# Four projections by rows of 256 columns become two of 512 in both mixers, the rotation two units sooner

## The reference

```python
for layer in range(DEPTH):                      # DEPTH = 2
    h = rms_norm(x, attn_norm_w[layer])
    proj = h @ w_in[layer]                      # 1024 -> 3072 columns, 12 slices of 256
    a_q, a_i, a_zf, a_zb, a_g, b_u, c_q, c_k, c_v = jnp.split(proj, SPLIT_POINTS, axis=-1)
    o_a = hgrn2_mixer(a_q, a_i, a_zf, a_zb, a_g, lb_all[layer])     # a chunkwise scan, 256 wide
    o_b = fourier_mixer(b_u)                                        # 2-D DFT, 256 wide
    o_c = dilated_attention_mixer(c_q, c_k, c_v, positions)         # rotary + attention, 512 wide
    x = x + jnp.concatenate([o_a, o_b, o_c], -1) @ w_out[layer]
    ...                                         # feed-forward
```

## Time and profile before

| | us |
|---|---|
| median of 3 runs | 2207.61 |
| lowest and highest run | 2207.59, 2208.95 |
| span of the profiled execution, first to last instruction | 2211.8 |
| PE busy in the span | 2148.4 (97%) |
| DVE, ACT, POOL busy | 1324.7, 949.9, 189.1 |

### The profile page before, as it was taken

The page is one execution under the profiler, slowest core; times in us unless marked ns, Lnnn a source line. Parts: engine busy times, 40 slices in busy tenths (PEclk is TensorE's granted clock), DMA queues, the critical chain, the costliest instruction groups (busy, mean ns, idle before and its releaser), DMA issues.

```text
span 2211.8 us, 32932 instructions
## 1 busy us (share of the span) xinstructions
PE 2148.4 (97%) x13984; PEld 1681.6 (76%) x13984; DVE 1324.7 (60%) x1976; ACT 949.9 (43%) x1442; POOL 189.1 (9%) x159
## 2 busy tenths in 40 slices
PE   8998999999999999999999999999999998999997
PEld 6885688888888785788888885676888567777775
DVE  8886555335437867455255453857433454888887
ACT  5445532222234347432223332345221234888885
POOL 1220000000001310100000200000000001122220
PEclk9999999999999999999999999999999998999999
DMA  5222033322222231222222221212110443799985
GB/s 187 69 80 77 20 119 119 119 101 97 102 85 77 72 96 39 76 83 102 102 96 95 96 96 55 77 53 82 59 59 32 144 168 125 292 349 364 358 346 217
DMA packets 55000, 275.69 MB, mean 125 GB/s; under 512 B 13142, under 2 KB 13398, under 8 KB 26048
## 3 DMA queue, kind: packets, MB, share of 16 engines
q1 hardware_dynamic: 45344, 264.32, 33.0%
q0 software_dynamic: 8928, 8.33, 1.1%
q10 hardware_dynamic: 576, 0.87, 0.1%
HBM read 268.31 MB, written 29.36 MB: 135 GB/s over the span
## 4 chain that ended last, share of the span: by engine, by line
PE 86%; DVE 7%; ACT 3%; DMA 1%; issue 1%; SPq 0%; POOL 0%; POOLq 0%; DVEq 0%; ACTq 0%
PE psum L123 83%; PE psum L126 3%; DVE A_mix L136 2%; ACT A_mix L130 1%; DVE WL L136 1%; DMA A_moe<-h_rows,A_moe 1%; ACT A_mix L133 1%; DVE A_second L136 1%; DVE A_mix L156 0%; DVE A_second L144 0%; DVE A_mix L162 0%; ACT WH L130 0%; SPq L168 0%; DMA A_mix<-A_mix 0%; DVE HL L136 0%
## 5 line engine op out<-in xcount | busy, mean ns | idle before, releaser
L136 DVE TENSOR_TENSOR WL<-raw,WH 128x1024 fp32r<-128x1024 f32 x236 | 300.9, 1277 | 351.6 <-ACT WH L130 351.2
L130 ACT ACTIVATE WH<-raw 128x1024 fp32r<-128x1024 f32 x236 | 247.5, 1054 | 357.6 <-PE psum L123 341.7
L123 PE MATMUL psum<-HH,WH 128*128 128x512 f32 x736 | 301.6, 410 | 17.5 <-DVE HL L144 10.1
L123 PE MATMUL psum<-R_op,WH 128*128 128x512 f32 x1024 | 316.0, 390 | 0.0
L123 PE MATMUL psum<-R_ffn,WH 128*128 128x512 f32 x1024 | 315.1, 389 | 0.0
L123 PE MATMUL psum<-HH,WL 128*128 128x512 f32 x736 | 290.3, 394 | 0.0
L123 PE MATMUL psum<-HL,WH 128*128 128x512 f32 x736 | 290.2, 394 | 0.0
L123 PEld LDWEIGHTS psum<-R_op,WH 128*128 128x128 f32 x1024 | 192.2, 188 | 40.6 <-issue 1.0
L123 PEld LDWEIGHTS psum<-R_ffn,WH 128*128 128x128 f32 x1024 | 192.2, 188 | 39.9
L123 PE MATMUL psum<-R_moe 128*128 128x512 f32 x800 | 198.3, 404 | 5.8 <-DVE ring_moe L136 3.4
L123 PE MATMUL psum<-R_ffn,WL 128*128 128x512 f32 x512 | 199.2, 389 | 0.0
(11 more groups left out here) (206 smaller groups left out, 3000.1 us busy)
## 6 DMA issues: line engine op xcount, KB each, us to landing
ring_moe<-in_w_gu SPq DMA_DIRECT2D x64, 1024.0 KB, 10.1
raw<-in_w_in SPq DMA_DIRECT2D x41, 1024.0 KB, 5.0
raw<-in_w_up SPq DMA_DIRECT2D x32, 1024.0 KB, 4.9
raw<-in_w_down SPq DMA_DIRECT2D x32, 1024.0 KB, 4.9
ring_moe<-in_w_dn SPq DMA_DIRECT2D x32, 1024.0 KB, 6.8
raw<-in_w_out SPq DMA_DIRECT2D x12, 1024.0 KB, 4.9
kept<-A_second SPq DMA_DIRECT2D x20, 256.0 KB, 2.6
A_mix<-A_mix SPq DMA_DIRECT2D x64, 64.0 KB, 2.0
```

Of the source, the lines that this page charges most:

```text
L123: return self.raw.matmul(o, l, r, start=start, stop=stop)
L130: return self.raw.activation(o, i, f, scale=scale)
L136: return self.raw.tensor_tensor(o, a, b, op)
```

## The change

The two halves of the row lins are joined: a_i and b_u become one lin of 512 columns, c_v another, with weights from a new array `w_row` that holds 4 x 128 rows by 512 columns in a chunk. The order of the mixer's lins is now four of `head` (units 0 to 7), c_q and c_k by columns (8 to 15), a_i with b_u (16 to 19), c_v (20 to 23). A tile of 128 positions fills one bank, so a row lin uses all four banks 0 to 3; in its last unit PE takes the tiles in the order 2, 3, 0, 1, and ACT reads them out in that order. `ROT` falls from 14 to 12. In `MIX` the scan's step kt moves behind two more half-units on ACT.

```diff
-                      lin([W[0, 0]], "silu", m.aq2, ly=ly), lin([W[4, 0]], "silu", m.ag2, ly=ly),
-                      lin([W[1, 0]], "rows", m.ai3, ly=ly)]
+                      lin([W[0, 0]], "silu", m.aq2, ly=ly), lin([W[4, 0]], "silu", m.ag2, ly=ly)]
...
-            m.tail += [lin([W[5, 0]], "rows", m.u3, ly=ly)]
-            m.tail += [lin([W[10 + j, 0]], "rows", m.cv3[:, :, 256 * j:256 * j + 256], ly=ly) for j in range(2)]
+            for j, to in enumerate(((m.ai3, m.u3), (m.cv3,))):
+                m.tail.append(lin([I["w_row"][ly, j, k] for k in range(2)], "rows", to, ly=ly))
...
-            for m in range(2):
-                b = (2 * (l.n - s2.low[0].n) + m) % 3 if l.kind in ("lat", "shift", "keep") else l.n % 2 * 2 + m
+            for m in range(4 if l.kind == "rows" else 2):
+                b = (2 * (l.n - s2.low[0].n) + m) % 3 if l.kind in ("lat", "shift", "keep") else (l.n % 2 * 2 + m) % 4
...
+        ROWS = (2, 3, 0, 1)
+
         def pe_rows(e, l):
...
+            us = [chunks[n][2] + h for n in l.chunks for h in range(2)]
+            for i, u in enumerate(us):
+                e.wait_ge(*at("w_lo", u))
+                wh, wl = unit(u)
+                final = u == us[-1]
+                order = ROWS if final else (0, 1, 2, 3)
+                for tk in order:
+                    if i == 0:
+                        clear(e, l, tk)
+                    o, ts = bank_of(l, tk), slice(tk * 128, (tk + 1) * 128)
+                    for k in range(2):
+                        xh, xl, made = operand(l, 2 * i + k)
+                        e.wait_ge(*at(*made))
+                        ws = slice(k * 512, (k + 1) * 512)
+                        e.mm(o, xh[:, ts], wh[:, ws], i + k == 0, False)
+                        e.mm(o, xl[:, ts], wh[:, ws], False, False)
+                        t = e.mm(o, xh[:, ts], wl[:, ws], False, final and k == 1)
...
+            if l.kind == "rows":
+                e.wait_ge(*at("nrm_dve", 2 * l.ly - 1, "col"))
+                for tk in ROWS:
+                    ps, w = bank_of(l, tk), S // len(l.to)
+                    e.wait_ge(*at("lin_mm", l.n, tk))
+                    for i, to in enumerate(l.to):
+                        t = e.act(to[:, tk, :], ps[:, i * w:(i + 1) * w], ACT.Copy, rcol[:, tk:tk + 1])
+                    t.then_inc(*did("lin_act", "ps", l.n, tk))
+                return
...
-            e.wait_ge(*at("lin_act", "ps", x.head[4].n, 1))
+            e.wait_ge(*at("lin_act", "ps", x.tail[4].n, 1))
...
-                    l = x.tail[-1 if part else -2]
-                    e.wait_ge(*emptied(l, 1))
-                    e.wait_ge(*emptied(x.tail[-1], 1))
+                    e.wait_ge(*emptied(x.tail[-1], 1 if part else 3))
...
-        ROT = 14
+        ROT = 12
...
-        MIX = "u" * 12 + "c" + "uu" + "cucuu" * 8 + "cuu" * 4 + "cuuuc"
+        MIX = "u" * 12 + "c" + "uu" + "cucuu" * 8 + "cuuuu" + "cuu" * 2 + "c" + "cuuuc"
```

More of the change, by code:

```diff
@@ new lines, in pe_rows @@
+            us = [chunks[n][2] + h for n in l.chunks for h in range(2)]
[15 more added lines that the diff above has]
+                        t = e.mm(o, xh[:, ts], wl[:, ws], False, final and k == 1)
+                    if final:
+                        t.then_inc(*did("lin_mm", l.n, tk))
+                    elif tk == 3:
+                        t.then_inc(*did("w_use", u))
+                    if tk in (order[1], order[3]):
+                        yield
@@ L606, in act_made @@
                     e.act(sg, sg if l.kind == "gate" else l.to[:, m, :], ACT.Sigmoid).then_inc(*did("lin_act", "sg", l.n, m))
[L607 to L613, removed]
                 elif l.kind == "copy":
@@ L1494, in win_dve @@
             for i, also in ((21, fold), (22, fold_again)):
-                steps[f"s{i}"] = lambda i=i, also=also: (rot_dve(e, x, i - ROT), also(e, x))
+                steps[f"s{i}"] = lambda also=also: also(e, x)
             yield from between(dve_lins(e, x.head + x.tail, True), **steps)
@@ L3287, in layout @@
     a["w_down"] = np.stack([lay(g["w_down"][i], 8, 256) for i in range(2)])
+    a["w_row"] = np.stack([lay(np.concatenate([w[:, 256:512], w[:, 1280:1536], w[:, 2560:3072]], 1), 4, 512)
+                           for w in (g["w_in"][i] for i in range(2))])
     q = {k[:-2]: x[0] for k, x in g.items() if k.endswith("_2")}
```

## The result

The changed kernel takes **2244.24 us** (median of 4 executions, 2242.90 to 2248.69) where the kernel before takes 2208.28 (2207.59 to 2211.77): ratio 1.016, 95% interval 1.0145 to 1.0175, slower by 36.0 us.

A forecast was written before the change was run, and what follows sets the result against it. PE, busy 97%, was taken as the bound, with DVE near its limit. Terms summed to +14.1 us a mixer, +28.2 for two: span 2240.0, median 4.2 lower, 2236 us, slower by 1.3%; range 2219 to 2246.

The forecast's parts named there:

- Bank 2 at unit 16: PE in unit 16 waits 7.5 us for ACT's late read-out, plus 1.5 for DVE's earlier rotation: 9.0 us.
- The clock, and between: After unit 16's standstill, half clock costs 2.3 us; up to the fifteenth level step PE saves 0.6.
- Sum to the fifteenth step: Up to the fifteenth level step, a mixer: -0.4 + 7.5 + 1.5 + 2.3 - 0.6 = +10.3 us.
- kt behind the last chunk: kt's copies stand behind unit 22's split; st ends 25.6 us after the fifteenth step: +5.3, slow clock +1.0.
- The matmul form: Row lins: 192 double-width matmuls replace 384, saving 0.013 us a pair, 1.6 to 2.6 us a mixer if PE bounds.
- Behind: After st: st to o 8.5 us instead of 9.6, -1.1; o to the DFT -1.4.
- Sum for a mixer: Whole mixer: 10.3 + 5.3 + 1.0 - 1.1 - 1.4 = +14.1 us; two mixers +28.2.
- 1 and 2: Rivals: only the bank waits cost, 2223 us, chance 0.13; only kt's wait costs, 2213 us, chance 0.07.
- Rival 3: Faster: PE stays the bound throughout, about -3.9 us a mixer, 2200 us; chance 0.05.
- Rival 4: The gains and part of a wait cancel, within 0.2% or 4.4 us; chance 0.04.
- rival 5: Worse: DVE meets POOL (3.4 us) and both standstills bring full slow stretches, or attention slips in; 2242 to 2248; chance 0.11.

The follow-up runs named there:

- the filled run: Changed kernel plus 34 unused matmuls of 128x512 into an idle bank, just ahead of the wait for bank 2 in unit 16: 2244.50 us.
- both orders mended: Changed kernel with ACT's read-out of units 14 and 15 ahead of the sixth level's exponentials and kt's copies ahead of unit 22's split: 2211.94 us.
- the second and first runs: On the changed kernel: kt's copies ahead of unit 22's split, 2229.02 us (second); read-out of units 14 and 15 ahead of sixth-level exponentials, 2226.79 us (first).

## Why the prediction was right, and where it was short

- **Bank 2 at unit 16** (forecast -0.4 + 7.5 + 1.5 = 8.6): PE restarts at 133.26 in place of 123.85, 9.4. The missing 0.8 is DVE, which let the exponentials start 2.3 us later (130.47 against 128.16) and not 1.5; it lies within the bounds of 0 and 3.4. In DVE's six operations ahead of the exponentials, 0.72 us of it is a wait for a swap to land, which the forecast did not have, and 1.1 is a longer run of the six beside POOL (4.77 us for 3.70). The mechanism is shown by the run that moves this read-out alone: the 8.8 us go, and 17.5 us of the whole.
- **The clock, and between** (forecast 2.3 - 0.6 = 1.7): 15.64 us from restart to fifteenth step in place of 138.02 - 123.85 = 14.17, so 1.5. The slow stretch is 1.9 by the filled run. By the rule of the Trainium skill that I had set beside it (TensorE: Matmul & The Clock Gate, "HAM oscillation — how this bites in real kernels") a wait for data that is long enough has the array throttled again, and what follows starts slow. The trace agrees: 0.51 in the standstill, half speed behind it, and 1.00 again from 139 us.
- **Sum to the fifteenth step**: forecast +10.3, measured 148.90 - 138.02 = +10.9.
- **kt behind the last chunk** (forecast 5.3 + 1.0): **this is the term that was too small.** The distance from the fifteenth step to ACT's split held (forecast 21.6, now 169.80 - 148.90 = 20.9). But "PE would reach st at 20.3 and then stand 3.4 us" is wrong: PE had to stop before it came to st. The scan turns on three banks, its fourth group of transposes needs the bank that ACT's first copy of kt frees, and a half-unit is queued behind it. St is through at 177.89 - 148.90 = 29.0 us, not 25.6: 8.7 in place of 6.3. Some 1.4 of the 8.7 is the half clock behind the wait (the half-unit from 172.14 to 176.34 takes 4.20 us, the one at full clock from 161.78 to 164.62 takes 2.84), close to the 1.0 allowed for it; so the order of the rows costs 7.3 and not 5.3. Bank 7 for that group brings back 24.9 in the first mixer and 26.2 in the second, where st waits 3.07 us for the copies, as the forecast had it (3.4). I had moved the copies behind the chunk and looked for who waits for their data (st), not for who waits for their banks.
- **The matmul form**: the step between level steps is 142.14 - 138.10 = 4.04 us as forecast. PE's busy time is 3.8 us less, and nothing is gained, since PE is no longer what bounds here. The 3.8 is no clean measure of the form: busy time grows where the clock is low, and in four of the runs with both orders mended it is 2136.7 to 2141.5 us, 7 to 12 below the kernel before, with no shorter time of the whole.
- **Behind**: st to o is 8.4 us (forecast 8.5), o to the DFT 16.3 in place of 17.8 (forecast -1.4, measured -1.6), and the DFT's wait is gone.
- **Sum for a mixer**: forecast +14.1, at the DFT +16.85. Two mixers: forecast 28.2, 32.5 at the root of the second block. The medians differ by 36.0, the spans of the two profiled executions by 29.6. The difference between the two figures comes from how single executions spread: in the profiled execution of the changed kernel and of each run the span is 1.7 to 2.0 us shorter than the time of that execution, so the profiled one of the kernel before (span 2211.8), whose time is not on record, took about 2213.6 us, 5.3 above its median, while that of the changed kernel (2243.15) lies 1.1 below its own; 29.6 + 5.3 + 1.1 = 36.0. So the 4.2 us that the prediction took off the span were no fixed difference of span and time, but the distance of one slow execution from the median. The last 3.5 us, from 32.5 to 36.0, need no row of their own.
- **The rivals**: 1 and 2 are what the second and first runs make by hand: with only the bank wait 2229 (I gave 2223), with only kt 2227 (I gave 2213, since kt's part was under-sized and I took the DVE and unit 20 waits for nothing). Rival 3 falls: even with both waits mended the form's gain is eaten by waits of 1 us for DVE and the one at unit 20, and the kernel is at best level. Rival 4 falls with the 36.0. The measured 2244 lies in the stretch of rival 5 (2242 to 2248), and a half of that rival came true: both standstills were followed by half clock, but DVE's lateness was 2.3 and not 3.4, and the larger part of what the forecast lacks is the bank of the transposes, which no rival names. The range held the time by 1.8 us only, and its upper end came from what was allowed for the clock and for DVE, not from the term that was missed: that it held is in part luck.

No run shows that `ROT` had to fall with the new order of lins. By the code, with 14 the last chunk would stand behind swaps whose rotation DVE reaches only behind the split of unit 22, which needs that chunk, and the engines would wait for each other.

## What to carry to other kernels

A wider tile that fills a bank also doubles how many banks a group opens at once; look up when each was last read out, and what stands ahead of that read-out in the list of the engine that does it. When a copy out of PSUM is moved later, ask both who needs its data and who needs its bank: the second may stand earlier in PE's list. And before spending effort on PE's instruction form, see that its in-order partners leave it something to run: here 3.8 us of PE's busy time went, and 36 us were lost, 32 of them to two rows in ACT's order.

## What was not expected of the hardware

A wait of about 2 us can be followed by half clock or by none. In the run with bank 7 the matmuls behind a wait of 1.97 us start every 0.43 us for some 3 us (granted clock 0.62 from 164 to 168 us); in the run with `ROT = 11` the same wait, 1.95 us at the same place, leaves the clock at 1.00. It differs within one execution as well: with both orders mended the wait of 1.94 us at unit 20 of the first mixer is followed by 2.80 us for the next half-unit, the wait of 1.96 us at the same place of the second mixer by 4.16. In the ten executions of that kernel the fastest (2209.48 us) has a mean granted clock of 0.993 and the slowest (2217.70) one of 0.987. So low clock and long time go together here; that single waits decide it is likely, not shown. It fits that an edit worth 1 us shows in the trace but not in the median.
